# Dilated attention by pairs of heads, masked biases made ahead, projections and gate inside its first and last steps, output matrices split around the norm

## What is computed

```python
def dilated_attention_mixer(h, w_in, w_out, rel_bias):
    proj = h @ w_in                       # q, k, v for 3 groups x 16 heads x 64, and the gate z
    for g, (window, dilation) in enumerate(((128, 1), (512, 4), (2048, 16))):
        # query t attends to t - j*dilation: logits q.k/8 + bias(distance, head), masked; out and log-sum-exp
        ...
    wts = softmax(stack(lses), axis=0)    # the three groups are weighted by their sums
    o = sum(wts * outs)
    return (o * silu(z)) @ w_out

x = x + rms_norm(dilated_attention_mixer(rms_norm(x, g1), ...), g2)
x = x + rms_norm(s5_mixer(rms_norm(x, g3), ...), g4)
```

## Time and profile before

| | us |
|---|---|
| median of 3 runs (2367.21 to 2367.39) | 2367.23 |
| the profiled execution | 2363.95 |
| its span | 2362.1 |
| PE busy | 2008.4 (85% of the span) |
| DVE / ACT / POOL busy | 642.6 / 397.3 / 373.6 |
| chain that ended last, share PE / DVE / issue / DMA / ACT / POOL | 77 / 8 / 8 / 3 / 3 / 1% |

### The profile page before, as it was taken

One profiled execution on the slowest core, in us unless ns is written; L12 is line 12 of the kernel. 1 busy time (PEld: TensorE's weight loads), 2 busy tenths in 40 slices (PEclk: granted clock), 3 DMA queues, 4 the chain that ended last, 5 costly groups with the idle time before them and its releaser, 6 DMA issues.

```text
span 2362.1 us, 28984 instructions
## 1 busy us (share of the span) xinstructions
PE 2008.4 (85%) x12318; PEld 1145.3 (48%) x12318; DVE 642.6 (27%) x1345; ACT 397.3 (17%) x839; POOL 373.6 (16%) x282
## 2 busy tenths in 40 slices
PE   4989969988988737999969888888669999995898
PEld 3567444444443215456533333333257677672775
DVE  2234241111111133113331101111252320387152
ACT  2133220000000002022220000000021321331131
POOL 1124330000000011023320000000100200237030
PEclk8999979999999978999979999999889999997899
DMA  9248139999999955225449999999664324333221
GB/s 369 94 157 304 76 111 427 424 424 425 425 426 425 423 226 177 69 87 209 172 175 425 425 422 425 425 420 424 259 220 143 109 72 143 108 99 115 73 83 54
DMA packets 139088, 594.41 MB, mean 252 GB/s; under 512 B 19332, under 2 KB 30612, under 8 KB 105024
## 3 DMA queue, kind: packets, MB, share of 16 engines
q1 hardware_dynamic: 113168, 557.86, 59.3%
q10 hardware_dynamic: 19600, 28.07, 3.5%
q0 software_dynamic: 6176, 6.42, 0.8%
HBM read 582.71 MB, written 21.65 MB: 256 GB/s over the span
## 4 chain that ended last, share of the span: by engine, by line
PE 77%; DVE 8%; issue 8%; DMA 3%; ACT 3%; POOL 1%; SPq 0%; POOLq 0%; ACTq 0%; DVEq 0%
PE banks L1325 19%; PE banks L1350 10%; PE banks L2127 7%; PE banks L1302 5%; PE banks L1719 4%; PE banks L1056 4%; PE banks L2129 3%; PE banks L563 3%; PE banks L1721 2%; PE banks L2465 2%; PE banks L324 2%; PE banks L817 1%; PE banks L341 1%; PE banks L805 1%; PE banks L676 1%
## 5 line engine op out<-in xcount | busy, mean ns | idle before, releaser
L1325 PE MATMUL banks<-RG,HT 128*64 128x512 f32 x2112 | 485.5, 613 | 88.2 <-issue 86.0
L1325 PEld LDWEIGHTS banks<-RG,HT 128*64 128x64 f32 x2112 | 173.0, 141 | 388.1 <-issue 385.0
L1454 POOL DMA_INDIRECT y_rows<-AR x66 | 64.4, 976 | 907.5 <-DVE AR L1354 894.6
L1334 DVE TENSOR_TENSOR AR<-AR,banks 128x256 f32<-128x256 f32 x66 | 39.7, 602 | 557.9 <-ACT AR L1330 497.3
L2127 PE MATMUL banks<-HT,RG 128*128 128x256 f32 x768 | 166.9, 379 | 0.7 <-ACT HT L443 0.7
L1330 ACT ACTIVATE AR<-banks 128x256 f32<-128x256 f32 x66 | 25.3, 383 | 789.5 <-PE banks L1325 789.5
L2127 PEld LDWEIGHTS banks<-HT,RG 128*128 128x128 f32 x768 | 145.8, 190 | 22.5 <-issue 2.1
L1302 PE MATMUL banks<-AR 128*128 128x256 bf16 x1152 | 149.3, 278 | 3.4 <-DVE AR L1291 3.4
L1302 PEld LDWEIGHTS banks<-AR 128*128 128x128 bf16 x1152 | 109.7, 100 | 62.7 <-issue 49.0
L1350 PE MATMUL banks<-RG,AR 128*64 128x512 f32 x528 | 120.6, 599 | 2.6 <-DVE AR L1343 2.6
L1350 PE MATMUL banks<-AR 128*64 128x512 f32 x528 | 120.6, 599 | 2.6 <-DVE AR L1343 2.6
(11 more groups left out here) (377 smaller groups left out, 2502.1 us busy)
## 6 DMA issues: line engine op xcount, KB each, us to landing
RG<-in_moe_w SPq DMA_DIRECT2D x165, 2048.0 KB, 19.6
AR<-in_moe_w SPq DMA_DIRECT2D x33, 2048.0 KB, 22.0
RG<-in_ada_w SPq DMA_DIRECT2D x24, 2048.0 KB, 8.2
RG<-in_attn_w_in SPq DMA_DIRECT2D x20, 2048.0 KB, 7.8
RG<-in_odd_w_in SPq DMA_DIRECT2D x6, 2048.0 KB, 16.6
RG<-in_ssm_w_in SPq DMA_DIRECT2D x4, 2048.0 KB, 7.9
AR<-y_rows ACTq DMA_DIRECT2D x6, 1024.0 KB, 9.1
RG<-in_even_w_in SPq DMA_DIRECT2D x2, 2048.0 KB, 20.3
```

Source lines behind the costliest of these rows:

```text
L1325: m = pe.matmul(p[64 * h:64 * h + 64, :], x[:, k, :], w[:, :, k, 256 * h:256 * h + 256], start=k == 0, stop=k == 7)
L1454: g.indirect_dma_start(y, off, E.Y[b], None, bounds_check=2047, oob_is_err=False).then_inc(*event)
```

## The change

The class `Attention` and its five functions are gone. `Pairs` now takes, for every unit, lists of scores, blocks, turns and buffers, and serves all three attentions. For the dilated one:

- A unit is two heads and a query tile: 8 units a half, t = 0 and 1 in turn. The two heads' scores contract over 64 partitions each and are issued in turn; q is stored once and no zeros are written. For t = 0 the heads use banks 0 and 1; for t = 1 they lie side by side over banks 2 to 4 and share the middle one, so PE waits (`second_begun`) before it writes the part of the first head that falls there. Turns (groups of up to four transposed blocks) take banks 5 and 6 by turns, ACT copying from 5 and DVE from 6; the values use bank 7. The transposed probabilities have one buffer.
- Bias and maximum are one DVE instruction (`tensor_tensor_reduce`) per head.
- Weighing is on POOL, except one head of each t = 0 unit, which is on ACT.
- The masked biases of all 8 heads of a half are made in one go by POOL, in the first half as soon as mask and biases are there, in the second after the last maximum of the first.
- The last two of the 30 projection parts (v of group 2) run within steps 0 and 1 of the half's attention. The first six parts of the second half, and the first six of the eight gate parts, run within the last three steps (two a step) of the first and second attention; parts 0 and 1 wait for the exponentials of unit 6, parts 2 and 3 for those of unit 7, parts 4 and 5 for the bank's copy.
- The gate has four buffers, and POOL's multiplication waits only for the unit it needs.
- `dve_outputs` does the beginning and m = 1, 2 ahead of the norm, and m = 3, 4 after it, in `dve_ssm`; ACT no longer waits for them. `pe_direct` waits for m = 3.
- In the first attention of the first block DVE waits for `gain2_load` after 12 of the `between` steps and not ahead of all.

```diff
         def pe_pairs(pe, A, between):
             N, name = len(A.units), A.name
@@ -672,32 +686,42 @@
                     u = A.units[s]
                     if s >= 2:
                         pe.wait_ge(*at("exped", name, s - 2, 1))
-                    for x in range(2):
-                        m = pe.matmul(PS[2 * (s % 2) + x][:, 0:u["n"]], u["q"][x], u["k"][x], start=True, stop=True)
+                    for g in range(len(u["scores"][0])):
+                        for x in range(2):
+                            q, k, o = u["scores"][x][g]
+                            if u["shared_bank"] and (g, x) == (2, 0):
+                                pe.wait_ge(*at("second_begun", name, s))
+                            m = pe.matmul(o, q, k, start=True, stop=True, skip_group_check=True)
+                            if u["shared_bank"] and (g, x) == (0, 1):
+                                m.then_inc(*ev("second_begun", name, s))
                     m.then_inc(*ev("scores", name, s))
                 next(between, None)
                 if s >= 3:
                     i = s - 3
                     u = A.units[i]
+                    for k in range(len(u["turns"])):
+                        pe.wait_ge(*at(*A.turned_out(i, k)))
...
                     for j in range(nb):
                         for x in range(2):
-                            m = pe.matmul(PS[6][64 * x:64 * x + 64, 0:128], u["v"][x][j],
-                                          A.PT[x][:, 128 * j:128 * j + 128], start=j == 0, stop=j == nb - 1)
+                            m = pe.matmul(PS[A.out_bank][64 * x:64 * x + 64, 0:128], u["v"][x][j], u["pt"][x][j],
+                                          start=j == 0, stop=j == nb - 1)
                     m.then_inc(*ev("values", name, i))
                 next(between, None)
                 if 0 <= s - 2 < N:
+                    u = A.units[i]
+                    for k, turn in enumerate(u["turns"]):
+                        for x in sorted({x for x, _ in turn.blocks}):
+                            pe.wait_ge(*at(*A.weighed(i, x)))
+                        if k >= 2:
+                            pe.wait_ge(*at(*A.turned_out(i, k - 2)))
+                        for y, (x, j) in enumerate(turn.blocks):
+                            m = pe.transpose(PS[turn.bank][:, 128 * y:128 * y + 128],
+                                             u["pb"][x][:, 128 * j:128 * j + 128], IDN[:])
+                        m.then_inc(*ev("probs_turned", name, i, k))
...
         def act_pairs(act, A, between):
...
+                    for k, turn in enumerate(A.units[i]["turns"]):
+                        if turn.on_act:
+                            act.wait_ge(*at("probs_turned", name, i, k))
+                            if i:
+                                act.wait_ge(*at("values", name, i - 1))
+                            act.activation(turn.to, PS[turn.bank][:, 0:128 * len(turn.blocks)],
+                                           ACT.Copy).then_inc(*ev("probs_act", name, i, k))
+                if 0 < s <= N:
+                    u = A.units[s - 1]
+                    for x in range(2):
+                        if u["weigh_act"][x]:
+                            act.wait_ge(*at("inverse", name, s - 1))
+                            act.activation(u["pb"][x], u["pb"][x], ACT.Copy, scale=A.small_of(s - 1, 3)[:, x:x + 1]).then_inc(
+                                *ev("weighed_act", name, s - 1, x))
                 if s < N:
                     u = A.units[s]
                     act.wait_ge(*at("shift", name, s))
+                    if s >= 3:
+                        act.wait_ge(*at("probs_turned", name, s - 3, len(A.units[s - 3]["turns"]) - 1))
...
+                        act.activation(u["pb"][x], u["z"][x], ACT.Exp, bias=A.small_of(s, 1)[:, x:x + 1], scale=u["scale"],
                                        accum_out=A.small_of(s, 2)[:, x:x + 1]).then_inc(*ev("exped", name, s, x))
...
+                    if nb:
+                            if "mask" in u:
+                                v.wait_ge(*at("mask", *u["mask"][x]))
+                            z = like(u["z"][x][:, 0:nb], u["bias"][x])
+                            ins = v.tensor_tensor_reduce(out=z, in0=z, in1=u["bias"][x], scale=1.0,
+                                                         scalar=top[:, x:x + 1] if nb < u["n"] else -3.0e38, op0=ADD,
+                                                         op1=MAX, accum_out=top[:, x:x + 1])
                         vstep(v, ins)
...
         def dve_even_between(v):
+            for x, _ in enumerate(dve_ada(v, 0, ada_second(0), mods0, GB)):
+                if x == 11:
+                    v.wait_ge(*at("gain2_load", 0))
+                yield
             v.wait_ge(*at("ab1_load"))
...
+        DIL_EARLY, DIL_LATE = 6, 28
...
+        def dil_bank(n):
+            return n % 4 if n < DIL_LATE else n - DIL_LATE + 6
...
+        def dil_units(hh):
+            units, groups = [], 0
+            for a in range(4):
+                for t in range(2):
+                    i, kn = len(units), 128 * (t + 1)
+                    n = 3 * kn
+                    if t == 0:
+                        z = [PS[x][:, 0:n] for x in range(2)]
                     else:
+                        flat = PSA[:, 2:5, :].rearrange("p a b -> p (a b)")
+                        z = [flat[:, n * x:n * x + n] for x in range(2)]
+                    pt = [[PT2[:, 128 * (3 * (t + 1) * x + j):128 * (3 * (t + 1) * x + j) + 128] for j in range(3 * (t + 1))]
+                          for x in range(2)]
+                    blocks = [(x, j) for x in range(2) for j in range(3 * (t + 1))]
+                    turns = []
+                    for b0 in range(0, len(blocks), 4):
+                        own = blocks[b0:b0 + 4]
+                        turns.append(Turn(own, 5 + groups % 2, groups % 2 == 0, PT2[:, 128 * b0:128 * (b0 + len(own))]))
+                        groups += 1
+                    hl = [2 * a + x for x in range(2)]
+                    units.append(dict(
+                        scores=[[(Q3[g][64 * x:64 * x + 64, a, 128 * t:128 * t + 128], K3[64 * x:64 * x + 64, g, a, 0:kn],
+                                  z[x][:, g * kn:g * kn + kn]) for g in range(3)] for x in range(2)],
+                        z=z, n=n, scale=1.0, biased=n, mask=[(hh, h) for h in hl],
+                        pb=[PB2[i % 3][:, n * x:n * x + n] for x in range(2)],
+                        v=[[V3[:, j, g, 64 * h:64 * h + 64] for g in range(3) for j in range(t + 1)] for h in hl],
+                        o=OT2[:, 4 * hh + a, 128 * t:128 * t + 128], pt=pt, turns=turns, weigh_act=(False, t == 0), shared_bank=t == 1))
+            return units
...
+        def pe_dil_between(pe, hh):
+            for n in range(DIL_LATE, 30):
+                pe_dil_part(pe, hh, n)
+                yield
+                yield
+            for j in range(2):
+                pe.wait_ge(*at("dil_out_act", hh, 2, 2, j))
+            for _ in range(12):
+                yield
+            for n in range(DIL_EARLY):
+                if hh == 0:
+                    pe_dil_part(pe, 1, n)
                 else:
+                    pe_gate_part(pe, n)
+                yield
...
+            g.wait_ge(*at("dist_out", 15))
             for hh in range(2):
                 if hh:
+                    g.wait_ge(*at("shift", "dil0", 7))
+                for h in range(8):
+                    g.tensor_tensor(BM[:, h], bc(BI[:, 8 * hh + h, :], 1, 3), DM, ADD).then_inc(*ev("mask", hh, h))
+                pool_pairs(g, A2[hh], iter(()))
...
+        ZS = [ar(19 * KK + 256 * i, 256) for i in range(4)]
...
+        def act_gate_part(act, n):
+            act.wait_ge(*at("gate_in", n // 4, n % 4))
+            if n >= 4:
+                act.wait_ge(*at("gated_out", n - 4))
+            act.activation(ZS[n % 4], PS[n % 4][:, 0:256], ACT.Silu).then_inc(*ev("gate_out", n))
         def pool_gate(g):
             for n in range(8):
                 g.wait_ge(*at("gate_out", n))
-                g.tensor_tensor(OT2[:, n, :], OT2[:, n, :], ZS[n % 2], MUL).then_inc(*ev("gated_out", n))
+                if n >= 4:
+                    g.wait_ge(*at("att_out", "dil1", 2 * (n - 4) + 1))
+                g.tensor_tensor(OT2[:, n, :], OT2[:, n, :], ZS[n % 4], MUL).then_inc(*ev("gated_out", n))
...
         def act_attended(act):
+            for n in range(DIL_EARLY, 8):
+                act_gate_part(act, n)
             act_turn_b(act)
+            act.wait_ge(*at("att_out", "dil1", 7))
             act.dma_start(YG[2], rows(I["attn_post_norm_2"][0])).then_inc(*dm("post_gain", 2))
-            act.wait_ge(*at("gated_out", 7))
             act.dma_start(PG2, rows(I["ssm_pre_norm_2"][0])).then_inc(*dm("ssm_gain"))
-            act.wait_ge(*at("outputs", 4))
             for t in range(2):
                 act_post(act, 2, t)
         def dve_attended(v):
+            dve_outputs_begin(v)
```

(26 more changed lines are left out.)

449 lines of the change are left out of this document (134 added, 315 removed).

## The result

The changed kernel takes 2328.2 us (median; 2325.9 to 2332.7, four runs) against 2367.2 (2364.2 to 2367.4, four) for the one before: ratio 0.984, 95% interval 0.982 to 0.986. The profiled execution took 2332.66 (span 2330.9), the slowest of the four; the profiled one before took 2363.95.

A forecast was written before the change was run, and what follows sets the result against it. PE was taken to bound projections and attentions, DVE and the serial norm chain the stages behind. 33.0 us up to the ssm's projections plus 5.8 in the first attention made 38.8: median 2328.4 from 2367.23, range 2317 to 2343.

The forecast's parts named there:

- Attention of the first block: First block's first attention: DVE's 4.3 us wait for the gain and the clock loss behind it go, 5.8 us (4.3 to 7.0).
- drain of some 0.2 us: Attention scores on PE: a tiling mode change drains the engine; if paid on top, 16 units would cost 3 us more.
- the slope from 384 and 512: POOL's weighing: 1.24 us for 384 elements and 1.56 for 512, extended along that line to 2.20 for 768.
- The round 9.0: Attention's middle: a loop of inverse, POOL, transposes, ACT's copy, weighing and exponentials takes 9.0 us per pair of units.
- the old rate: Rival: the attention loop stays at 11.3 us per pair of units, +13.8, 2342 us; chance 0.15.
- PE alone: Rival: PE's work alone sets the attention loop, middle 19.2 instead of 26.5 us, twice, 2314 us; chance 0.07.
- An attention 70.0 (16.7, 26.5, 26.9): Each half's attention, from the end of its last k part: lead 16.7, middle 26.5, tail 26.9 us.
- The rival of a clock at 1.2 GHz throughout: PE's clock falls throughout both attentions because of gaps in the middle: +110, 2438 us; chance 0.04.
- The wait for `wo`: Ahead of the norm: PE's 3.0 us wait for the second output weight piece grows to 6.6.
- about 107.5: Start of the norm's squares, at about 2107.5 us; quarter (0, 1) ends then instead of 2105.5 if the clock falls.
- DVE's outputs end: Ahead of the norm: DVE finishes 18 instead of 30 instructions at 2107 us, where it was 2141.5 before.
- The norm 39: Norm stage: its 38.1 us become 39, since POOL works beside it for 34 us instead of 30.

## Why the prediction was right

The forecast was 2328.4 and the time 2328.2; that close is luck, since the kernel's own runs spread over 6.8 us. The mechanism was right in nearly every step; one path in the middle of the attentions and the size of POOL's hold on the norm were not seen (times from the first part's start, forecast and then measured):

- Attention of the first block: 5.8 forecast, 5.3 measured, alone too.
- Scores 1.5 and 0.85 us forecast, 1.50 and 1.05 measured (0.9 to 0.95 without a wait), so no drain of some 0.2 us shows on top of them; values of a t = 1 unit 1.53, as forecast. POOL's 768 elements 2.20, measured 2.206: the slope from 384 and 512 held. The joint DVE pass 1.03, measured 0.98, and 0.14.
- The round 9.0: measured 8.85 and 9.16 between POOL's starts. The first is the loop of the prediction: POOL, transposes, ScalarE's copy, weighing and exponentials. In the second another path, which the prediction did not have, ends 0.8 us later: DVE's copy, the next unit's scores and their maxima, and only then the inverse. Two paths of nearly the same length gave one number. So halving POOL's part shortened PE's first round by 2.75 and left the second at 8.63. The rivals "the old rate" and "PE alone" are excluded.
- An attention 70.0 (16.7, 26.5, 26.9): measured 71.3 (16.9, 27.0, 27.4). The excess is the middle's clock, 1.3 us: behind PE's first wait for POOL, scores and values of one unit took 3.8 us (1870.45 to 1874.28) where the next round's take 2.5. The rival of a clock at 1.2 GHz throughout had its place but not its size: 0.94 in the middles, 1.00 beside them.
- The projections around them, 110.7 and 90.0: 110.7 and 89.9.
- The wait for `wo`: 6.6 forecast, 5.7 measured; SP's 24 issues 11.9 (12.5), the transfer 13.0 (12.9). The products on it took 8.7 instead of 6.9, the first four or five of the 16 instructions at the lower clock (0.86 us apart instead of 0.43), which the text had allowed for with "about 107.5". Squares 371.9 forecast, 374.0 measured: the two attentions are 2.6 later and the shorter issues give 0.5 back.
- DVE's outputs end: 371.4 forecast, 371.5 measured, 2.5 ahead of the squares. Both were nearly the bound, which is why moving the weights alone brought 1.3 by stage.
- The norm 39: 38.3. The part of it that was not seen: 15.2 of these are POOL's doing, line by line. It cancelled in the difference, since the kernel before paid it too (38.1).
- From first part to ssm: 33.0 less forecast, 31.8 measured.

The sum by stages is 31.8 + 5.3 = 37.1. The profiles differ by 31.3, since the profiled execution after lost 3 us at the start of the odd attention (2.08 and 5.83 us in the rows above, 1.13 and 3.72 in the profile before) and 3 in the last stage's two groups of products (30.4 and 29.4 against 28.9 and 27.7); the medians differ by 39.0. So 38.8 was too high by 1.7 in its stages. The profiled execution before was 3.3 faster than its median, and the one after 4.4 slower; what gave the 1.7 back in the medians is not shown, and it is less than the runs spread.

## What to carry to other kernels

When two engines meet at one point, price the two halves of a change together and each alone: here 7.2 and 5.2 us alone, 31.8 together. When a measured round agrees with the loop that you computed, look at a second one: here another path was within 1 us, and shortening the first alone gave less than expected. Look at what a busy GpSimd does to short VectorE instructions on the path; the busy share hides it, while the duration of the same line with and without it shows it. Where runs of one kernel spread by 0.3%, a gain of 6 us can vanish in the medians and still be read from a stage of the profile that nothing else touches.

## What was not expected of the hardware

- DVE beside POOL's instructions on 1024 elements: 128 x 1 instructions with two inputs in SBUF 0.17 alone and up to 2.2 (they end with POOL's), those with one input 0.17 in both; 1024-element ones with two inputs 1.22 and 3.26. POOL's own 2.35 becomes 3.21 beside the latter.
- TensorE's granted clock behind the very same gap ahead of the odd attention (PE idle for 1.71 us): of twelve profiles without products in it, one kept 2.4 GHz (the one before: 1.13 and 3.72 us), six lost 1.6 us (the lower level, 1.2 GHz, began or ended inside the next 16 products) and five lost 3.0 (2.08 and 5.8 us). With products in the gap both profiles kept it.
- Two products in different row halves overlap when they alternate in the stream (1.50 us for three pairs of 256 columns) and don't when the halves follow one another (3.1).
